# Conditioning blocks dealt out anew between the recurrent heads and the first ConvFFN of a two-layer diffusion step

## The reference

```python
def trunk_layer(x, mod, l, p, init, rows):
    shift1, scale1, gate1, shift2, scale2, gate2 = jnp.split(mod[:, None, :], 6, axis=-1)
    xn = rmsnorm(x, p['norm_mix_pre'][l]) * (1.0 + scale1) + shift1
    ...
    x = x + gate1 * rmsnorm(y, p['norm_mix_post'][l])
    xn = rmsnorm(x, p['norm_ffn_pre'][l]) * (1.0 + scale2) + shift2
    y = conv_ffn(xn, p['ffn_w_in'][l], p['ffn_conv_w'][l], p['ffn_conv_b'][l], p['ffn_w_out'][l], rows)
    x = x + gate2 * rmsnorm(y, p['norm_ffn_post'][l])
```

## Time and profile before

| | |
|---|---|
| median of 3 runs | 3657.24 us (3656.77 to 3657.71) |
| the profiled execution's own time | 3658.1 us |
| its span, first to last instruction | 3656.4 us |
| PE busy | 3240.8 us (89%) |
| DVE busy | 2219.6 us (61%) |
| POOL busy | 995.9 us (27%) |
| ACT busy | 798.7 us (22%) |
| mean granted TensorE clock | 0.938 of full |

### The profile page before, as it was taken

One profiled execution on the slowest core, in us unless ns is written; L12 is line 12 of the kernel. 1 busy time (PEld: TensorE's weight loads), 2 busy tenths in 40 slices (PEclk: granted clock), 3 DMA queues, 4 the chain that ended last, 5 costly groups with the idle time before them and its releaser, 6 DMA issues. The chain is left out here.

```text
span 3656.4 us, 47222 instructions
## 1 busy us (share of the span) xinstructions
PE 3240.8 (89%) x18299; PEld 3144.6 (86%) x18299; DVE 2219.6 (61%) x2703; ACT 798.7 (22%) x1518; POOL 995.9 (27%) x435
## 2 busy tenths in 40 slices
PE   8788888886979999999987898897788999999995
PEld 8678778876979999999977887786788999999995
DVE  1555558773267777777765242545147677777775
ACT  1433331222031111111104233333113111111110
POOL 1221122221213333333421211111212334334430
PEclk8899899998999999999988998898999999999997
DMA  4112223332211111111112110101231111111112
GB/s 185 45 63 73 72 75 128 124 126 77 91 66 35 45 41 40 41 45 40 40 64 88 32 39 24 39 26 36 88 127 31 40 40 40 42 44 40 40 40 104
DMA packets 86232, 226.60 MB, mean 62 GB/s; under 512 B 8016, under 2 KB 45136, under 8 KB 85888
## 3 DMA queue, kind: packets, MB, share of 16 engines
q1 hardware_dynamic: 44208, 164.21, 13.9%
q10 hardware_dynamic: 41936, 61.17, 4.9%
HBM read 194.94 MB, written 30.41 MB: 62 GB/s over the span
## 5 line engine op out<-in xcount | busy, mean ns | idle before, releaser
L726 PE MATMUL bank<-xh,wh 128*128 128x384 f32 x3888 | 1353.6, 348 | 101.0 <-DVE xl L2116 35.5
L726 PE MATMUL bank<-xl,wh 128*128 128x384 f32 x3888 | 1330.9, 342 | 0.0
L726 PE MATMUL bank<-xh,wl 128*128 128x384 f32 x3888 | 1329.1, 342 | 0.0
L707 POOL TENSOR_TENSOR wh<-raw,ones 128x1024 fp32r<-128x1024 f32 x206 | 420.5, 2041 | 2559.5 <-PE bank L726 2524.0
L726 PEld LDWEIGHTS bank<-xh,wh 128*128 128x128 f32 x3888 | 756.4, 195 | 130.9 <-issue 81.7
L726 PEld LDWEIGHTS bank<-xl,wh 128*128 128x128 f32 x3888 | 755.6, 194 | 0.5
L726 PEld LDWEIGHTS bank<-xh,wl 128*128 128x128 f32 x3888 | 753.1, 194 | 0.0
L2137 DVE SCALAR_TENSOR_TENSOR cc<-pad,cw,cc 128x1024 f32<-128x1024 f32 x352 | 608.6, 1729 | 11.8
L709 POOL TENSOR_TENSOR wl<-raw,wh 128x1024 fp32r<-128x1024 f32 x206 | 570.2, 2768 | 16.2
L726 PE MATMUL bank<-hh,wh 128*128 128x384 f32 x1056 | 362.1, 343 | 31.1 <-DVE hl L2147 16.2
L726 PE MATMUL bank<-hl,wh 128*128 128x384 f32 x1056 | 360.7, 342 | 0.0
(11 more groups left out here) (239 smaller groups left out, 2868.2 us busy)
## 6 DMA issues: line engine op xcount, KB each, us to landing
raw<-in_w SPq DMA_DIRECT2D x206, 512.0 KB, 3.5
ada_w<-in_ada SPq DMA_DIRECT2D x56, 512.0 KB, 3.7
residual_scratch<-y ACTq DMA_DIRECT2D x9, 1536.0 KB, 5.7
xg<-residual_scratch ACTq DMA_DIRECT2D x9, 1536.0 KB, 8.5
ada_x<-in_ada SPq DMA_DIRECT2D x24, 512.0 KB, 3.6
xr<-mixer_scratch ACTq DMA_DIRECT2D x16, 576.0 KB, 3.7
front<-in_ada SPq DMA_DIRECT2D x16, 512.0 KB, 7.7
y<-in_x SPq DMA_DIRECT2D x1, 4608.0 KB, 21.6
```

What stands on the lines that cost most here:

```text
L707: nc.gpsimd.tensor_tensor(wh[s][:, :], raw[s][:, :], ones[:, 0:1].broadcast_to([128, 1024]), ALU.mult).then_inc(w_hi[s], 1)
L726: return nc.tensor.matmul(out, lhsT, rhs, start=start, stop=stop)
```

## The change

The 80 blocks made on DVE are dealt out anew. An mLSTM head makes 6 instead of 7, a retention head (the first three) 10 instead of 16, and each of the 11 turns of the first ConvFFN makes 2: 4 + 24 + 30 + 22 = 80. In the ConvFFN they stand on DVE after `finish()` and `set_taps`, ahead of the taps of tile 0, with a new buffer `ada_y` beside `ada_w`. SP's turn of the ConvFFN loads the first after its third weight block and the second after its fourth. In the heads SP's strings and the places of `more` follow the new counts. And `front_even(0)` waits for the third bank only, whose last user is the projection block before, and so no more for the second group of the gate projection.

```diff
-ADA_MLSTM = 7
-ADA_RET = 16
+ADA_MLSTM = 6
+ADA_RET = 10
+ADA_FFN = 2
...
+        ada_y = sb("ada_y", [128, 1024], scope=ffn_scope)
+        macc_y = sb("macc_y", [128, ADA_FFN, 2], scope=ffn_scope)
...
+                        elif name == "ffn0":
+                            sp.wait_ge(x_new, 3)
+                            ada_two(turn * na + (a0 + c), c, ada_y)
                             c += 1
...
-            stream("head0", 1, "awawaawaawa")
-            stream("mlstm", 3, "awawaawaawa")
-            stream("ret", 3, "aawaaawaaaaawaaaawaa")
+            stream("head0", 1, "awawaawaaw")
+            stream("mlstm", 3, "awawaawaaw")
+            stream("ret", 3, "aawaaawaawaaaw")
             stream("last", 1, "w")
             stream("out0", 3, "ww")
-            stream("ffn0", FP, "wwwwww")
+            stream("ffn0", FP, "wwwawaww")
...
                 if g == 0:
-                    for c in range(3):
-                        pe.wait_ge(pj_free[c], n.before(pj_free[c]))
+                    pe.wait_ge(pj_free[2], n.before(pj_free[2]))
...
-                    if t in (1, 3, 5):
-                        more(1 if mlstm else 2)
+                    if t in ((1, 4) if mlstm else (1, 3, 5)):
+                        more(1)
...
-                more(1 if mlstm else 2)
+                more(1)
                 for g in range(3):
                     (front_mlstm if mlstm else front_ret)(g)
                     if g == 2 or not mlstm:
-                        more(2 if g == 2 and not mlstm else 1)
+                        more(1)
                 states_even(mlstm, more)
-                more(2 if mlstm else 4)
+                more(2 if mlstm else 3)
...
                 set_taps(turn)
                 for _ in range(4):
                     act_takes(slot())
+                if layer == 0:
+                    for j in range(ADA_FFN):
+                        ada(j, 1 - j, ada_y, cc[1][:, 0:1024], macc_y)
+                    conditioning(turn * ADA_FFN + (96 - FP * ADA_FFN), ADA_FFN, macc_y)
                 for tap in range(12):
                     conv_tap(0, tap)
```

More of the change, by code:

```diff
@@ L125 @@
  'dve.ffn0': {'a_padded': 2,
+              'ada_loaded0': 16,
+              'ada_loaded1': 16,
+              'ada_used': 2,
               'conv_done': 2,
-              'dve_order': 23,
+              'dve_order': 24,
               'gelu_done': 2,
@@ L162 @@
               'w_used1': 3},
- 'dve.mlstm': {'ada_loaded0': 112,
-               'ada_used': 7,
+ 'dve.mlstm': {'ada_loaded0': 96,
+               'ada_used': 6,
                'dve_order': 33,
@@ L221 @@
              'z_logs': 2},
- 'dve.ret': {'ada_loaded0': 128,
-             'ada_loaded1': 128,
-             'ada_used': 16,
+ 'dve.ret': {'ada_loaded0': 80,
+             'ada_loaded1': 80,
+             'ada_used': 10,
              'dve_order': 19,
@@ L311 @@
  'pool.split': {'raw_loaded0': 16, 'raw_loaded1': 16, 'w_hi0': 1, 'w_hi1': 1, 'w_used0': 1, 'w_used1': 1},
- 'sp.ffn0': {'w_ready0': 3, 'w_ready1': 3},
+ 'sp.ffn0': {'ada_used': 2, 'w_ready0': 3, 'w_ready1': 3},
  'sp.ffn1': {'w_ready0': 3, 'w_ready1': 3},
- 'sp.mlstm': {'ada_used': 7, 'w_ready0': 2, 'w_ready1': 2},
+ 'sp.mlstm': {'ada_used': 6, 'w_ready0': 2, 'w_ready1': 2},
  'sp.odd': {'w_ready0': 3, 'w_ready1': 3},
@@ L317 @@
  'sp.out1': {'w_ready0': 1, 'w_ready1': 1},
- 'sp.ret': {'ada_used': 16, 'w_ready0': 2, 'w_ready1': 2}}
+ 'sp.ret': {'ada_used': 10, 'w_ready0': 2, 'w_ready1': 2}}
 class Tally:
@@ L421, in build @@
         vv = [sb(f"vv{t}", [128, T], scope=ffn_scope) for t in range(2)]
-        sb("under_norm", [128, TG + KT * TG - 2 * T], scope=ffn_scope)
+        ada_y = sb("ada_y", [128, 1024], scope=ffn_scope)
+        macc_y = sb("macc_y", [128, ADA_FFN, 2], scope=ffn_scope)
+        sb("under_norm", [128, TG + KT * TG - 2 * T - 1024 - 2 * ADA_FFN], scope=ffn_scope)
         heads_scope = ExitStack()
@@ L611, in ada, with ada_two @@
                 sp.dma_start(ada_w[:, :], a["ada"][n]).then_inc(ada_loaded[0], 16)
-            def ada_two(n, c):
+            def ada_two(n, c, other):
                 sp.wait_ge(ada_used, seen.before(ada_used) - 1)
@@ L617, in ada_two @@
                 s = (c + 1) % 2
-                sp.dma_start((ada_x if s else ada_w)[:, :], a["ada"][n]).then_inc(ada_loaded[s], 16)
+                sp.dma_start((other if s else ada_w)[:, :], a["ada"][n]).then_inc(ada_loaded[s], 16)
             def stream(name, turns, pattern):
@@ L630, in once @@
                         elif name == "ret":
-                            ada_two(turn * na + (a0 + c), c)
+                            ada_two(turn * na + (a0 + c), c, ada_x)
+                            c += 1
+                        elif name == "ffn0":
+                            sp.wait_ge(x_new, 3)
+                            ada_two(turn * na + (a0 + c), c, ada_y)
                             c += 1
@@ L1857, in boundary, with ada @@
                 lower(2)
-            def ada(j, s=0):
+            def ada(j, s=0, other=ada_x, spare=junk[:, :], sums=macc):
                 dve.wait_ge(ada_loaded[s], n.next(ada_loaded[s], 16))
@@ L1863, in ada, with conditioning @@
                     dve.wait_ge(ada_used, n.before(ada_used))
[L1864 to L1867, removed]
+                w = (other if s else ada_w)[:, :]
+                v.tensor_tensor_reduce(spare, w, crows[:, 0, :], 1.0, 0.0, ALU.mult, ALU.add, sums[:, j, 0:1])
+                v.tensor_tensor_reduce(w, w, crows[:, 1, :], 1.0, 0.0, ALU.mult, ALU.add, sums[:, j, 1:2]).then_inc(ada_used, 1)
                 n.next(ada_used)
-            def conditioning(column, count):
+            def conditioning(column, count, sums=macc):
                 dve.wait_ge(ada_used, n.before(ada_used))
-                link(v.tensor_tensor(mod[:, bass.ds(column, count), :], macc[:, 0:count, :],
+                link(v.tensor_tensor(mod[:, bass.ds(column, count), :], sums[:, 0:count, :],
                                      b3(ada_b[:, bass.ds(column, count)], 2), ALU.add))
@@ L2192, in finish, with pair @@
                 low(1)
-            def pair(turn, with_down, saved=0):
+            def pair(layer, turn, with_down, saved=0):
                 if with_down:
@@ L2217, in ffn @@
                 dve.wait_ge(conv_loaded, n.next(conv_loaded, 16))
-                pair(0, False, saved=48 if layer == 0 else 3 * 48)
+                pair(layer, 0, False, saved=48 if layer == 0 else 3 * 48)
                 with n.loop(dve, f"dve.ffn{layer}", FP - 1) as turn:
-                    pair(turn + 1, True)
+                    pair(layer, turn + 1, True)
                 finish()
@@ L2278, in _ @@
             with n.loop(dve, "dve.ret", 3) as turn:
-                head_even(False, turn, turn * ADA_RET + 48)
+                head_even(False, turn, turn * ADA_RET + (ADA_FRONT + ADA_GATES + 4 * ADA_MLSTM))
             head_even(False, 3, None)
+            assert ADA_FRONT + ADA_GATES + 4 * ADA_MLSTM + 3 * ADA_RET + FP * ADA_FFN == 96
             passes(4 + 7 * 4 + 1)
```

## The result

The changed kernel takes 3769.9 us (median of 4 runs, 3767.9 to 3775.1) against 3657.2 us; the ratio is 1.031, with a 95% interval of 1.0292 to 1.0328. That is 113 us slower. The forecast was 3783 us. The profiled execution has a span of 3766.2 us, 109.8 more than before.

What follows compares the result with a forecast made beforehand. PE's work plus its waits were taken to bound the kernel. From the profiled 3658.1 us, 35 gained in the heads and 161 lost in the ConvFFN gave 3784.1, or 3783 us after the 0.9 us median offset; range 3748 to 3826.

Steps and rivals of the forecast that it cites:

- The phase of SP: ConvFFN: the second conditioning block is issued behind weight block 6p+3, after PE finishes 6p-1; first tap 24.8 us later.
- The stall: ConvFFN turns 1 to 10: PE waits 13.6 us a turn for a bank, because late taps hold up ACT.
- the slope from before: ConvFFN taps: 0.73 us lost for each us of POOL split beside them, 3.1 us in turn 2.
- the full lock of the port: ConvFFN taps: DVE shut out by POOL for the whole split, losing 4.3 us instead of 3.1; total 12 us higher.
- the clock: ConvFFN: PE runs at 0.50 for some 4.5 us after each stall, costing 2.5 us a turn.
- What comes after: ConvFFN after the stall: down projection and taps of tile 1 are not late a second time.
- The heads: mLSTM heads gain 10 us, three retention heads 24, the last 1: 35 us together, bounds 20 and 45.
- The gate wait: Even fronts' wait for the gate's evacuation goes away: 2.5 us in four mLSTM heads, 8.0 us in four retention heads.
- (1): Rival, ConvFFN: data come in time and the added work is hidden; 3622 us, chance 0.06.
- (2): Rival, ConvFFN: the stall drags a second behind it, 22 to 24 us a turn; about 3850 us, chance 0.07.
- (3): Rival, heads: they give back nearly nothing, neighbouring waits replacing each; 3808 us, chance 0.81 together with the forecast.
- (4): Rival, ConvFFN: stall shorter, about 10 us, the clock hardly falling; 3732 us, chance 0.06.

Runs made afterwards that it cites:

- the kernel that has this edit alone: Kernel before with 10 instead of 16 conditioning blocks in each of three retention heads, 18 columns left out or zero: 3620.6 us, ratio 0.99.
- another order: Changed kernel with both ConvFFN conditioning blocks loaded behind the turn's second weight block instead of the third and fourth: 3614.6 us, ratio 0.9884.

## Why the prediction was right, point by point

**The phase of SP, which decided the sign.** Forecast was that the second block of a turn is issued 0.53 us behind weight block 6p+3, lands 4.3 us later, and that DVE's taps wait for it. Measured in turn 2: issued 0.59 us behind, used 4.5 us after issue. From turn 1 on each turn has the stall. The experiments show the cause by dose: stall 13.4 to 14.3 us in ten turns as made, 4.4 to 5.6 in nine with both blocks one weight block earlier, none with both a place further ahead, none with a turn ahead, at the same DVE work.

**The stall.** Taps from 1187.09 to 1202.99, 15.9 us against a forecast of 15.5. The split beside them cost 3.5 us; the slope from before gave 3.1 and the full lock of the port 4.3. That this term came out so near is partly luck: the split took 5.7 us (1187.17 to 1192.90), not 4.3, and cost 0.61 us for each of its us, not 0.73. POOL was slowed too (a first pass of 2.43 us at 1187.17 against 1.89).

The Trainium skill, "SBUF — State Buffer", section "SBUF: two separate sides", says that DVE and GpSimd share one pair of ports under an exclusive lock, which the instruction that starts first holds for its whole length. That both engines lose time agrees with it; the 3.5 us that DVE lost beside 5.7 us of split are less than shutting it out for the whole split would cost, and no run here follows the lock instruction by instruction.

Stall 13.4 to 14.3 us against 13.6. For the clock PE was busy 77.9 us in the turn instead of 75.3, 2.6 us against 2.5, and 91.3 - 75.3 = 16.0 us a turn against 16.1. From the first stall to the end 160.9 us were lost against 161; the ConvFFN alone lost 163.5. What comes after was not late a second time: DVE waited for PE at the first addition of the down projection, as forecast.

**The heads.** This is the term that was mis-sized: 35 us forecast, 51 up to the first stall in the profile, 54 by the runs. The match of the total, 3783 against 3770, would have been closer with the right size here. The three retention heads became 12.7, 10.2 and 9.6 us shorter, where some 8 were forecast. Two parts were too small. I left 5 us of waits a head on gate, keys and queries; the changed kernel has 4.6, 3.0 and 3.0. And 1.5 us a head for the clock was an estimate from windows of the ConvFFN; the heads' busy time fell by 4.3 us a head in the kernel that has this edit alone. One piece of it can be seen in the kernel before, in which PE comes out of the wait of 3.98 us on states with twice the time for a product:

```profile
608.70 0.67 PE L726 MATMUL bank<-xh,wh 128*128 128x384 f32 x1
609.17 0.52 PE L726 MATMUL bank<-xl,wh 128*128 128x384 f32 x1
```

In the mLSTM heads 10 us were forecast and 15.6 came (383.5 us from 178 to the last transposes became 367.8): the waits on states fell by 10.2 us instead of 8.1, since one of the two that were to stay went too, the head norm gave the 2.5 us above, and the waits on `pr` (L1912, now L1920) fell from 19.6 to 17.4 us. The gate wait's gaps add up to 10.5 us; alone it is worth 3 to 6.

**The rivals.** (1), data in time, fell as the change stands, because both blocks came late as read; made true by an order a turn ahead, it gives 3603.5 us, where it was priced at 3622 with the 35 us for the heads. (2), a second stall, didn't come in the changed kernel; the later waits of its kind came small in another order (15.4 us in eight turns). (3), heads that give back, fell, but for the gate wait, where part of it came back. (4), a shorter stall, fell.

How much of the heads' 13 us of busy time is the clock alone, and how much how matmuls overlap at the gaps, stays open: the granted clock of the third head is 0.96 before with 69.9 us of busy time and 0.98 with 66.5 after, which is more than the clock's share. No run separates them.

## What to carry to other kernels

Before work is moved into a stage because an engine has idle time there, find at which point of that stage's loop the stream that feeds it stands. Here the loads stood in one queue behind weight loads that wait for PE to free a buffer, so they went out only when PE was already in the turn that needed them, and DVE, though free, waited. Issued a turn ahead, the same loads cost nothing that the runs show. And a gap is not the worth of a wait: the gate wait gave back less than its gaps, because the wait on the keys grew behind it, while fewer blocks in the retention heads gave more than the waits on states, in part because PE's busy time fell as well.

## What the runs showed of the hardware

PE's granted clock was 0.50 for 4.5 us after stalls of 13.5 us, no longer than after one of 8.0 us. Shorter waits cost clock too. In the kernel with both blocks one place earlier, after a stall of 4.74 us the first products ran at full speed, and the clock fell 0.7 us later: from 1753.76 to 1756.64 a product took 0.52 us instead of 0.34. After a stall of 5.24 us the products were slow from the first on.

```profile
1753.03 0.44 PE L736 MATMUL bank<-xh,wh 128*128 128x384 f32 x1 [4.74 <-ACT pad L1587]
1753.30 0.34 PE L736 MATMUL bank<-xl,wh 128*128 128x384 f32 x1
...
1754.08 0.52 PE L736 MATMUL bank<-xl,wh 128*128 128x384 f32 x1
...
1756.95 0.34 PE L736 MATMUL bank<-xl,wh 128*128 128x384 f32 x1
...
1835.47 0.69 PE L736 MATMUL bank<-xh,wh 128*128 128x384 f32 x1 [5.24 <-ACT pad L1587]
```

So a stall of 4.9 us on average still cost some 2 us of clock in a turn: PE was busy for 77.2 us from 1671.05 to 1753.03 in that kernel, against 75.3. The length of the wait alone doesn't tell whether the clock falls. In the changed kernel the transposes after a wait of 3.48 us and the products behind them ran at full speed; after a wait of 3.02 us in a retention head they didn't, and the granted clock was 0.50 from there to 716. After waits of 2.87 us in the ConvFFN with both blocks behind the second weight block it stayed at 1.00.

```profile
545.84 1.20 PE L933 MATMUL bank<-ident,num 128*128 128x128 f32 x9 [3.48 <-DVE num L1963]
546.80 0.42 PE L736 MATMUL bank<-xh,wh 128*128 128x384 f32 x1
...
712.27 0.90 PE L872 MATMUL bank<-ident,kT 128*128 128x128 f32 x3 [3.02 <-DVE kw L1928]
714.74 0.67 PE L736 MATMUL bank<-xh,wh 128*128 128x384 f32 x1
```
